# Dense up products: one matmul of 512 columns for both sides of the tokens, with a copy and a sum behind each group

## The chip, the cores and the metric

One core of one Trainium2 chip. The metric is device time in microseconds (us), from the start of the program on the core to its end. The kernel before ran three times: 1690.91 us in the median, 1690.83 to 1691.85. One further execution was profiled. It took 1693.8 us, of which 1691.8 us are the span from the first instruction to the last; all rows below come from it.

## The reference, cut to what matters

A decoder trunk of two layers over 256 tokens with 1024 features. Each layer has a mixer (attention and a recurrent branch), a feed-forward part and a small gated embedding. In layer 0 the feed-forward part is dense, in layer 1 it is a choice of experts. Only the dense one is touched:

```python
def swiglu(x, w1, w3, w2):
    return (jax.nn.silu(x @ w1) * (x @ w3)) @ w2

xn2 = rmsnorm(h, ffn_norm[0])
h = h + swiglu(xn2, dense_w1, dense_w3, dense_w2)   # w1, w3: 1024 x 3584, w2: 3584 x 1024
```

All data are 32-bit floats. The kernel keeps that precision on TensorE (PE) by splitting each operand into a rounded part ("hi") and its remainder ("lo") and adding three products: hi x hi, hi x lo and lo x hi.

## The kernel before, in words

**Weights.** SyncE (SP) loads weights from HBM in chunks of 2 MB into a ring of three slots `raw` (`load`, line 568); a chunk can be loaded when the chunk three before it has been split. A chunk is four quarters. The list `quarters` (line 148) names them in the order of their use. ScalarE (ACT) rounds quarter g into `w_hi` (`split_hi`, line 471), VectorE (DVE) subtracts to give `w_lo` (`split_lo`, line 482). There are six buffers of each, so the rounding of quarter g waits until the quarter g-6 has been read by PE (`wait_read`, line 457). Both engines call their splits through `Line.to(end)` (class `Line`, line 692), which emits the splits that are not yet emitted, up to but without the index `end`. So the place of a call of `hi.to` or `lo.to` in an engine's program is where its splits stand in that engine's order, and what is written ahead of them comes ahead of them.

**The dense part.** The 3584 hidden features are 7 chunks (c) of 4 tiles (ft), 28 groups. For each group i = 4c + ft PE multiplies one quarter of w1 and one of w3, eight k-tiles each, with the normed tokens, into the two halves of one PSUM bank: 2 x 8 x 3 matmuls of 256 columns (`split_product`, line 1175: `w_hi` with `xn_hi`, `w_hi` with `xn_lo`, `w_lo` with `xn_hi`). Groups take two banks `work` in turn. After the four groups of chunk c, PE multiplies with the four quarters of w2 of chunk c-1 (`down`, line 1337, 96 matmuls of 256 columns into `acc`), after the seventh chunk also with its own (`last_down`, line 1345). So the quarters stand in the order: eight of w1 and w3, (from the second chunk on) four of w2 of the chunk before, eight of w1 and w3, and so on.

**What follows a group** (`dense`, lines 950 and 1968; `last` is the index of the group's w3 quarter):

- ACT: `hi.to(last + 5)`; at the first group the root of the norm; wait for the scaled group; silu; `hi.to(last + 7)`.
- DVE: `lo.to(last + 5)`; at the first group the reciprocal of the root; wait for the group; multiply the bank of 512 columns by `rinv` into `up_buf` (line 1977; the profile names that space `gate_b`), which frees the bank; `lo.to(last + 7)`; wait for the silu; multiply, round to `hid_hi`, subtract to `hid_lo` (lines 1984, 1986, 1988).

Between groups of one chunk `last` grows by 2, so that `to(last + 5)` finds nothing left and `to(last + 7)` emits two quarters. Over w2's four quarters `last` jumps by 6: at the first group of the third to seventh chunk (c = 2 to 6) `to(last + 5)` emits four quarters, those of the groups ft = 1 and ft = 2 of that chunk. The group ft = 0 itself has its two quarters from before.

**The norm.** The root that the scaling needs is made from a sum that PE writes to the bank `misc` right after group 0 (`norm_root`, lines 1181, 767, 1732). The eight tiles `xn_hi` and `xn_lo` are made while the mixer's last products (`out`, eight groups of 24 matmuls) end; DVE adds each `out` bank to `hT`, which frees the bank.

Of the kernel before, what the change touches and what calls it, by code (L numbers as in the profile page):

```python
# [8 lines left out]
F32 = mybir.dt.float32  # L9
# [6 lines left out]
P = 128  # L16
D = 1024
T = 256
# [91 lines left out]
def trunk(nc, xT, pT, cols, rows, relT, wrg_d, wig_d, router_d, mix_w, dense_w, moe_w, ple_w, ple_p, bias_line, outT):  # L110
    groups = []
    for l in range(DEPTH):
        groups += [(l, *g) for g in mixer_groups()]
        if l % 2 == 0:
            groups += [(l, "ffn", c, ft) for c in range(FC) for ft in range(FT)]
        groups += [(l, "ple", j) for j in range(KT)]

    own = {g: (2 + TT * (g[2] - 1) + g[3], g[0]) for g in groups if g[1] == "qkv" and g[2]}
# [54 lines left out]
    with ExitStack() as ctx:  # L173
# [6 lines left out]
        def shared(name, n):  # L180

            with nc.sbuf_tensor(name, [P, n], F32) as plain:
                pass
            return plain, sb(name + "_r", [P, n], F32R)
# [3 lines left out]
        w_hi = [sb(f"w_hi{i}", [P, QUARTER], F32R) for i in range(UNITS_HELD)]  # L188
        w_lo = [sb(f"w_lo{i}", [P, QUARTER], F32R) for i in range(UNITS_HELD)]
        hT = sb("hT", [P, KT, T])  # L190
        x1, x1_r = shared("x1", KT * T)
        x2, x2_r = shared("x2", KT * T)
        areaA, areaA_r = shared("areaA", KT * T)
        areaB, areaB_r = shared("areaB", KT * T)
        areaK = sb("areaK", [P, KT * T])
# [60 lines left out]
        def squares_of(n):  # L256
            return areaA[:, 0:KT * T] if n % 3 == 0 else spare[:, KT * T:2 * KT * T]

        work_ps = [ctx.enter_context(nc.psum_tensor(f"work{i}", [P, 512], F32)) for i in range(2)]
        acc = [ctx.enter_context(nc.psum_tensor(f"acc{i}", [P, 1024], F32)) for i in range(2)]  # L260
        pv_ps = ctx.enter_context(nc.psum_tensor("pv_ps", [P, 512], F32))
        misc = ctx.enter_context(nc.psum_tensor("misc", [P, 512], F32))
        quad = [acc[0][:, 0:512], acc[0][:, 512:1024], acc[1][:, 0:512], acc[1][:, 512:1024]]
        work = [work_ps[0][:, :], work_ps[1][:, :]] + quad

        score_ps = acc[0][:, :].rearrange("p (h s) -> p h s", h=2)

# [31 lines left out]
        renormed = sem("renormed")  # L299
        ffn_bank = sem("ffn_bank")  # L300
        scaled = sem("scaled")
        ple_scaled = sem("ple_scaled")
        logits_taken = sem("logits_taken")
        logits_turned = sem("logits_turned")
# [152 lines left out]
        def wait_read(eng, g):  # L457

            l, _, _, _, by = quarters[g]
            if by[0] == "qkv":  # L460
                _, c, q = by
                if q < 3:
                    eng.wait_ge(rows_used, 9 * l + 3 * c + q + 1)
                else:
                    wait_full(eng, l, "qkv", c, TT - 1)
            elif by[0] == "w2":
                eng.wait_ge(ffn_acc, FC * FT * (l // 2) + FT * by[1] + by[2] + 1)
            else:
                wait_full(eng, l, *by)
# [24 lines left out]
        def wait_full(eng, l, *g):  # L494
            b, n = place[(l, *g)]
            eng.wait_ge(work_full[b], n + 1)

        def wait_taken(eng, l, *g):
            b, n = place[(l, *g)]
# [248 lines left out]
        def _(act):  # L748
# [201 lines left out]
            def dense(l):  # L950
                for i in range(FC * FT):
                    c, ft = divmod(i, FT)
                    last = q_at[((l, "w3", c), ft)]
                    hi.to(last + 5)
                    if i == 0:
                        norm_root(3 * l + 1)
                    act.wait_ge(scaled, FC * FT * (l // 2) + i + 1)
                    a = up_buf[:, i % 2, 0, :]
                    act.activation(a, a, ACT.Silu).then_inc(silu_ok, 1)
                    hi.to(last + 7)  # L960
                hi.to(phase_q[(l, "ple")] + 2)
                for k in range(KT):
                    if k == 6:
                        hi.to(phase_q[(l, "ple")] + 4)
                    norm_piece(3 * l + 2, k)
                hi.to(phase_q[(l, "ple")] + 5)
# [194 lines left out]
        def _(pe):  # L1161
# [167 lines left out]
            def dense(l):  # L1329
                def down_part(c, ft, j):  # L1330
                    g = q_at[((l, "w2", c), ft)]
                    hi, lo = unit(w_hi, g), unit(w_lo, g)
                    return split_product(quad[j // 2][:, T * (j % 2):T * (j % 2) + T], (hi[:, j, :], lo[:, j, :]),
                                         (hid_hi[:, c % 2, ft, :], hid_lo[:, c % 2, ft, :]),
                                         c == 0 and ft == 0 and j % 2 == 0, c == FC - 1 and ft == FT - 1)

                def down(c):
                    pe.wait_ge(hid_ok, FC * FT * (l // 2) + FT * (c + 1))
                    for ft in range(FT):
                        need(q_at[((l, "w2", c), ft)])  # L1340
                        for j in range(KT):
                            mm = down_part(c, ft, j)
                        mm.then_inc(ffn_acc, 1)

                def last_down():

                    c = FC - 1
                    for b in range(4):
                        for ft in range(FT):
                            if b == 0:  # L1350
                                pe.wait_ge(hid_ok, FC * FT * (l // 2) + FT * c + ft + 1)
                                need(q_at[((l, "w2", c), ft)])
                            for j in (2 * b, 2 * b + 1):
                                mm = down_part(c, ft, j)
                            if b == 3:
                                mm.then_inc(ffn_acc, 1)
                        if b < 3:
                            mm.then_inc(ffn_bank, 1)

                for c in range(FC):  # L1360
                    for ft in range(FT):
                        out = group_open(l, "ffn", c, ft)
                        for half, w in enumerate(("w1", "w3")):
                            g = q_at[((l, w, c), ft)]
                            need(g)
                            hi, lo = unit(w_hi, g), unit(w_lo, g)
                            for k in range(KT):
                                if c == 0 and ft == 0 and half == 0:
                                    pe.wait_ge(normed, KT * split_count(3 * l + 1) + k + 1)
                                mm = split_product(out[:, T * half:T * half + T], (hi[:, k, :], lo[:, k, :]),  # L1370
                                                   (xn_hi[:, k, :], xn_lo[:, k, :]), k == 0, k == KT - 1)
                        group_close(mm, l, "ffn", c, ft)
                        if c == 0 and ft == 0:
                            norm_root(3 * l + 1)
                    if c:
                        down(c - 1)
                last_down()
# [281 lines left out]
        def _(dve):  # L1659
# [308 lines left out]
            def dense(l):  # L1968
                for i in range(FC * FT):
                    c, ft = divmod(i, FT)  # L1970
                    last = q_at[((l, "w3", c), ft)]
                    lo.to(last + 5)
                    if i == 0:
                        norm_root(3 * l + 1)
                    wait_full(dve, l, "ffn", c, ft)
                    up = up_buf[:, i % 2, :, :]
                    taken(dve.tensor_tensor(up, bank_of(l, "ffn", c, ft).rearrange("p (h t) -> p h t", h=2),  # L1977
                                            rinv[:, :].unsqueeze(1).to_broadcast([P, 2, T]), ALU.mult), l, "ffn", c, ft)
                    wait_taken(dve, l, "ffn", c, ft)
                    dve.sem_inc(scaled, 1)  # L1980
                    lo.to(last + 7)
                    dve.wait_ge(silu_ok, FC * FT * (l // 2) + i + 1)
                    s = up[:, 0, :]
                    step(dve.tensor_tensor(s, s, up[:, 1, :], ALU.mult))
                    step.settle()
                    step(dve.tensor_copy(hid_hi[:, c % 2, ft, :], s))
                    step.settle()
                    dve.tensor_tensor(hid_lo[:, c % 2, ft, :], s, hid_hi[:, c % 2, ft, :].bitcast(F32),
                                      ALU.subtract).then_inc(hid_ok, 1)
                lo.to(phase_q[(l, "ple")] + 2)  # L1990
                for b in range(4):
                    if b < 3:
                        dve.wait_ge(ffn_bank, 3 * (l // 2) + b + 1)
                    else:
                        dve.wait_ge(ffn_acc, FC * FT * (l // 2 + 1))
                    dve.tensor_tensor(hT[:, 2 * b:2 * b + 2, :], hT[:, 2 * b:2 * b + 2, :],
                                      quad[b].rearrange("p (k t) -> p k t", k=2), ALU.add).then_inc(h_ffn, 1)
                    if b:
                        norm_piece(3 * l + 2, b - 1)
                norm_piece(3 * l + 2, 3)  # L2000
                lo.to(phase_q[(l, "ple")] + 5)
# [398 lines left out]
```

## Time and profile before

| | |
|---|---|
| median of 3 runs | 1690.91 us (1690.83 to 1691.85) |
| profiled execution | 1693.8 us, its span 1691.8 us |
| PE busy | 1671.0 us, 99% of the span |
| DVE, ACT busy | 1076.2 us (64%), 883.0 us (52%) |
| granted PE clock, mean over the span | 0.996 |
| dense part | about 250.4 to 494.4 us in the span |

PE is busy nearly everywhere. Matmuls overlap in their records, so that a busy PE does not say how fast they follow each other; for that one takes the distance of two starts. "x24" in a row means that 24 like instructions in a row were merged into one. "[3.38 <-PE work L1179]" means that the engine sat idle for 3.38 us before the instruction and what ended it. The clock is in shares of full speed (2.4 GHz).

### The profile page before, as it was taken

What the parts mean: (1) busy time and instruction counts of PE and PEld (TensorE: products, weight loads), DVE (VectorE), ACT (ScalarE), POOL (GpSimd) and SP (SyncE); (2) the same over time, 40 slices, a digit from 0 to 9 for tenths busy, and PEclk for the clock granted to TensorE, in tenths of its full rate; (3) what the DMA queues carried; (4) which work ended last, traced back from release to release, by engine and by line L of the source; (5) the groups of instructions that cost most, each with busy time, mean ns of one, the idle gap of its engine ahead of it and who ended that gap; (6) DMA issues with size and microseconds to landing.
All of it is one profiled execution on the core that took longest, in us unless ns stands there. A gap on an engine that the chain in (4) does not pass through costs nothing.

```text
span 1691.8 us, 26030 instructions
## 1 busy us (share of the span) xinstructions
PE 1671.0 (99%) x10246; PEld 1299.1 (77%) x10246; DVE 1076.2 (64%) x1662; ACT 883.0 (52%) x1349; POOL 18.6 (1%) x51
## 2 busy tenths in 40 slices
PE   9999999999999999998999999999999999999998
PEld 8888999999998988996666666666656666566557
DVE  7697876665668897866554555545555455555456
ACT  6778643433356678534534444445444455454444
POOL 3000000000000000000000000000000000000000
PEclk9999999999999999998999999999999999999999
DMA  9342453633544442435999999999999999999990
GB/s 336 144 163 100 166 215 153 243 153 150 210 188 150 156 157 106 170 156 190 417 417 388 417 412 409 418 392 414 410 410 417 412 394 410 411 417 413 394 383 27
DMA packets 62320, 485.98 MB, mean 287 GB/s; under 512 B 6880, under 2 KB 9200, under 8 KB 11504
## 3 DMA queue, kind: packets, MB, share of 16 engines
q1 hardware_dynamic: 62016, 484.09, 71.5%
q8 instruction: 84, 1.38, 0.3%
q14 instruction: 44, 0.36, 0.1%
q10 hardware_dynamic: 176, 0.15, 0.0%
HBM read 483.15 MB, written 1.07 MB: 286 GB/s over the span
## 4 chain that ended last, share of the span: by engine, by line
PE 95%; DVE 2%; DMA 1%; ACT 1%; issue 1%; POOL 0%; DVEq 0%; ACTq 0%; POOLq 0%
PE work L1177 17%; PE work L1178 16%; PE work L1179 16%; PE acc L1526 12%; PE acc L1177 6%; PE acc L1552 6%; PE acc L1179 6%; PE acc L1178 6%; PE acc L1258 1%; PE pv_ps L1488 1%; PE misc L1444 1%; PE misc L1442 1%; PE acc L1271 1%; PE misc L1426 1%; PE acc L1296 1%; PE misc L1435 1%
## 5 line engine op out<-in xcount | busy, mean ns | idle before, releaser
L2215 DVE TENSOR_TENSOR w_lo<-raw,w_hi 128x1024 fp32r<-128x1024 f32 x288 | 339.7, 1221 | 191.9 <-ACT w_hi L1005 186.6
L485 DVE TENSOR_TENSOR w_lo<-raw,w_hi 128x1024 fp32r<-128x1024 f32 x236 | 283.9, 1219 | 89.4 <-ACT w_hi L480 87.5
L1005 ACT ACTIVATE w_hi<-raw 128x1024 fp32r<-128x1024 f32 x288 | 288.2, 1050 | 55.0 <-DMA raw<-in_moe_w 51.6
L1177 PE MATMUL work<-x_r,w_hi 128*128 128x256 f32 x1024 | 297.0, 290 | 1.2 <-DVE gate_b L1977 0.7
L1178 PE MATMUL work<-x_r,w_hi 128*128 128x256 f32 x1024 | 289.5, 283 | 0.0
L1179 PE MATMUL work<-x_r,w_lo 128*128 128x256 f32 x1024 | 289.4, 283 | 0.0
L480 ACT ACTIVATE w_hi<-raw 128x1024 fp32r<-128x1024 f32 x236 | 241.8, 1048 | 67.8 <-PE acc L1179 29.1
L1526 PE MATMUL acc<-raw,bias 128*64 128x512 f32 x768 | 204.5, 598 | 0.0
L1177 PEld LDWEIGHTS work<-x_r,w_hi 128*128 128x128 f32 x1024 | 196.0, 191 | 8.9 <-issue 6.2
L1178 PEld LDWEIGHTS work<-x_r,w_hi 128*128 128x128 f32 x1024 | 196.1, 192 | 1.0 <-issue 0.7
L1179 PEld LDWEIGHTS work<-x_r,w_lo 128*128 128x128 f32 x1024 | 196.1, 192 | 0.0
L1177 PE MATMUL work<-w_hi,bias_r 128*128 128x512 f32 x448 | 182.7, 408 | 2.7 <-DVE w_lo L2215 2.7
L1178 PE MATMUL work<-w_lo,bias_r 128*128 128x512 f32 x448 | 175.7, 392 | 0.0
L1179 PE MATMUL work<-w_hi,bias_r 128*128 128x512 f32 x448 | 175.2, 391 | 0.0
L1526 PEld LDWEIGHTS acc<-raw,bias 128*64 128x64 f32 x768 | 58.6, 136 | 93.9 <-issue 93.9
L1177 PEld LDWEIGHTS work<-w_hi,bias_r 128*128 128x128 f32 x448 | 84.7, 189 | 41.2 <-issue 24.7
L1016 ACT ACTIVATE bias_r<-pv_ps 128x512 fp32r<-128x512 f32 x28 | 16.7, 597 | 171.2 <-PE pv_ps L1488 171.2
L1179 PEld LDWEIGHTS work<-w_hi,bias_r 128*128 128x128 f32 x448 | 84.7, 189 | 18.1
L1178 PEld LDWEIGHTS work<-w_lo,bias_r 128*128 128x128 f32 x448 | 84.8, 189 | 16.1
L1177 PE MATMUL acc<-w_hi,bias_r 128*128 128x512 f32 x224 | 93.3, 417 | 2.2 <-DVE w_lo L2215 2.2
L1552 PE MATMUL acc<-raw,lru 128*64 128x512 f32 x384 | 88.4, 598 | 0.0
L1179 PE MATMUL acc<-w_hi,bias_r 128*128 128x512 f32 x224 | 88.0, 393 | 0.0
(350 smaller groups left out, 2782.5 us busy)
## 6 DMA issues: line engine op xcount, KB each, us to landing
raw<-in_moe_w SPq DMA_DIRECT2D x288, 1024.0 KB, 10.5
raw<-in_mix_w SPq DMA_DIRECT2D x33, 2048.0 KB, 8.0
x<-in_moe_w SPq DMA_DIRECT2D x48, 1024.0 KB, 10.7
raw<-in_dense_w SPq DMA_DIRECT2D x21, 2048.0 KB, 8.2
raw<-in_ple_w SPq DMA_DIRECT2D x4, 2048.0 KB, 10.9
raw<-in_mix_w SPq DMA_DIRECT2D x4, 512.0 KB, 7.3
areaK<-in_ple_p SPq DMA_DIRECT2D x2, 1024.0 KB, 10.2
hT<-in_xT SPq DMA_DIRECT2D x4, 256.0 KB, 6.5
```

The source lines that it names most:

```text
L480: act.activation(unit(w_hi, g), raw_part(g), ACT.Copy).then_inc(hi_ok, 1)
L485: eng.tensor_tensor(unit(w_lo, g), raw_part(g), unit(w_hi, g).bitcast(F32), ALU.subtract).then_inc(split_ok, 1)
L1005: act.activation(w_hi[n % UNITS_HELD][:, :], heavy_quarter(where, c, j), ACT.Copy).then_inc(m_hi_ok, 1)
L1177: pe.matmul(out, stat[0], move[0], start=start, stop=False, skip_group_check=True)
L1178: pe.matmul(out, stat[0], move[1], start=False, stop=False, skip_group_check=True)
L1179: return pe.matmul(out, stat[1], move[0], start=False, stop=stop, skip_group_check=True)
L1258: mm = pe.matmul(score_ps[:, hh, 0:w], qT[HD * hh:HD * hh + HD, t, b * P:(b + 1) * P], kTT[HD * hh:HD * hh + HD, t // 2, 0:w], start=True, ...
L1271: mm = pe.transpose(acc[1][:, o:o + P], ebuf[:, u % 2, hh, P * kt:P * kt + P], ident[:, :])
L1296: mm = pe.matmul(quad[c % 4][HD * b:HD * b + HD, T * n:T * n + T], w[HD * b:HD * b + HD, c, :], xcT[HD * b:HD * b + HD, c, :], start=True, ...
L1526: mm = pe.matmul(quad[2][LIGHT * b:LIGHT * b + LIGHT, :], xg_light[:, k, :], w, start=(k == 0), stop=(k == KT - 1), skip_group_check=True)
L1552: mm = pe.matmul(quad[3][LIGHT * b:LIGHT * b + LIGHT, :], l_hid[:, ft, :], w, start=(c == 0 and ft == 0), stop=(c == FC - 1 and ft == FT - ...
L2215: dve.tensor_tensor(w_lo[u][:, :], heavy_quarter(where, n // HEAVY_C, n % HEAVY_C), w_hi[u][:, :].bitcast(F32), ALU.subtract).then_inc(m_s ...
```

## The change

Three things change, all for the dense part of layer 0:

1. `x1` and `x2`, which hold `xn_hi` and `xn_lo`, become halves of one buffer, so that one matmul can read both as 2 x 256 moving columns. For each quarter and k-tile PE now runs `w_hi` on [`xn_hi`, `xn_lo`] (512 columns) and `w_lo` on `xn_hi` (256 columns).
2. A group's result is now two sides of 256 columns for each of w1 and w3: 1024 columns, two banks. Even groups use both `work` banks, odd ones the banks of `pv_ps` and `misc`. ACT copies the second side to `up_buf`, DVE adds the first side to it (which frees the banks), then multiplies by `rinv`.
3. ACT and DVE put this copy, sum and scaling ahead of `to(last + 5)`, except at group 0. PE waits for both last `out` banks ahead of group 0, for the root (`rooted`) ahead of group 1, as that group writes to `misc`, and from group 2 on for the sum of the group two before.

```diff
-        x1, x1_r = shared("x1", KT * T)
-        x2, x2_r = shared("x2", KT * T)
+        x12, x12_r = shared("x12", 2 * KT * T)
+        x1, x1_r = x12[:, 0:KT * T], x12_r[:, 0:KT * T]
+        x2, x2_r = x12[:, KT * T:], x12_r[:, KT * T:]
+        xn_both = x12_r[:, :].rearrange("p (s k t) -> p k s t", s=2, k=KT)
...
+        def ffn_sides(i):
+            return (work_two, side_two)[i % 2][:, :].rearrange("p (h s t) -> p h s t", h=2, s=2)
...
 # ScalarE
                 for i in range(FC * FT):
                     c, ft = divmod(i, FT)
                     last = q_at[((l, "w3", c), ft)]
+                    if i == 0:
+                        hi.to(last + 5)
+                        norm_root(3 * l + 1)
+                    act.wait_ge(ffn_full, FC * FT * (l // 2) + i + 1)
+                    if i >= 2:
+                        act.wait_ge(hid_ok, FC * FT * (l // 2) + i - 1)
+                    act.activation(up_buf[:, i % 2, :, :], ffn_sides(i)[:, :, 1, :], ACT.Copy).then_inc(ffn_sided, 1)
                     hi.to(last + 5)
-                    if i == 0:
-                        norm_root(3 * l + 1)
                     act.wait_ge(scaled, FC * FT * (l // 2) + i + 1)
                     a = up_buf[:, i % 2, 0, :]
                     act.activation(a, a, ACT.Silu).then_inc(silu_ok, 1)
                     hi.to(last + 7)
...
 # TensorE
+                def up_product(out, hi, lo, k):
+                    pe.matmul(out[:, :, :], hi, xn_both[:, k, :, :], start=(k == 0), stop=False, skip_group_check=True)
+                    return pe.matmul(out[:, 0, :], lo, xn_hi[:, k, :], start=False, stop=(k == KT - 1), skip_group_check=True)
+
+                wait_taken(pe, l, "out", KT - 2)
+                wait_taken(pe, l, "out", KT - 1)
                 for c in range(FC):
                     for ft in range(FT):
-                        out = group_open(l, "ffn", c, ft)
+                        i = FT * c + ft
+                        if i == 1:
+                            pe.wait_ge(rooted, 3 * l + 2)
+                        elif i:
+                            pe.wait_ge(ffn_summed, FC * FT * (l // 2) + i - 1)
+                        out = ffn_sides(i)
...
-                                mm = split_product(out[:, T * half:T * half + T], (hi[:, k, :], lo[:, k, :]),
-                                                   (xn_hi[:, k, :], xn_lo[:, k, :]), k == 0, k == KT - 1)
-                        group_close(mm, l, "ffn", c, ft)
+                                mm = up_product(out[:, half, :, :], hi[:, k, :], lo[:, k, :], k)
+                        mm.then_inc(ffn_full, 1)
...
 # VectorE
+                    if i == 0:
+                        lo.to(last + 5)
+                        norm_root(3 * l + 1)
+                    up = up_buf[:, i % 2, :, :]
+                    both = ffn_sides(i)
+                    dve.wait_ge(ffn_sided, FC * FT * (l // 2) + i + 1)
+                    dve.tensor_tensor(up, up, both[:, :, 0, :], ALU.add).then_inc(ffn_summed, 1)
+                    dve.wait_ge(ffn_summed, FC * FT * (l // 2) + i + 1)
+                    dve.tensor_tensor(up, up, rinv[:, :].unsqueeze(1).to_broadcast([P, 2, T]), ALU.mult).then_inc(scaled, 1)
                     lo.to(last + 5)
-                    if i == 0:
-                        norm_root(3 * l + 1)
-                    wait_full(dve, l, "ffn", c, ft)
-                    up = up_buf[:, i % 2, :, :]
-                    taken(dve.tensor_tensor(up, bank_of(l, "ffn", c, ft).rearrange("p (h t) -> p h t", h=2),
-                                            rinv[:, :].unsqueeze(1).to_broadcast([P, 2, T]), ALU.mult), l, "ffn", c, ft)
-                    wait_taken(dve, l, "ffn", c, ft)
-                    dve.sem_inc(scaled, 1)
                     lo.to(last + 7)
```

## Rows read from the trace of the kernel before

**Rows 1.** The page's chain that ended last, shares by engine.

```profile
PE 95%; DVE 2%; DMA 1%; ACT 1%; issue 1%; POOL 0%; DVEq 0%; ACTq 0%; POOLq 0%
```

**Rows 2.** Windows, mid dense part: us, PE, PEld, DVE, ACT, POOL, PEclk, DMA, GB/s.

```profile
340.00:370.00 30.00, 30.00 (x252) 30.00 (x252) 16.76 (x23) 10.61 (x15) 0.00 (x0) 1.00 0.44 166
```

**Rows 3.** Timeline of PE: a matmul of group 24, and the first of group 25.

```profile
452.75 0.28 PE L1179 MATMUL work<-x_r,w_lo 128*128 128x256 f32 x1
...
453.95 0.28 PE L1177 MATMUL work<-x_r,w_hi 128*128 128x256 f32 x1
```

**Rows 4.** Timeline of PE in layer 1's first products, matmuls of 512 columns.

```profile
542.80 0.39 PE L1178 MATMUL acc<-w_lo,gate_a_r 128*128 128x512 f32 x1
...
544.61 0.39 PE L1177 MATMUL acc<-w_hi,gate_a_r 128*128 128x512 f32 x1
```

**Rows 5.** Timeline of DVE over a down product and the first group behind it.

```profile
442.46 2.56 DVE L485 TENSOR_TENSOR w_lo<-raw,w_hi 128x1024 fp32r<-128x1024 f32 x2
446.67 1.23 DVE L485 TENSOR_TENSOR w_lo<-raw,w_hi 128x1024 fp32r<-128x1024 f32 x1 [1.65 <-ACT w_hi L480]
449.55 1.23 DVE L485 TENSOR_TENSOR w_lo<-raw,w_hi 128x1024 fp32r<-128x1024 f32 x1 [1.65 <-ACT w_hi L480]
454.15 0.69 DVE L1977 TENSOR_TENSOR gate_b<-work,rinv 128x512 f32<-128x512 f32 x1 [3.38 <-PE work L1179]
```

**Rows 6.** Timeline of ACT over the same stretch.

```profile
437.98 2.94 ACT L480 ACTIVATE w_hi<-raw 128x1024 fp32r<-128x1024 f32 x3
...
448.45 1.06 ACT L480 ACTIVATE w_hi<-raw 128x1024 fp32r<-128x1024 f32 x1 [1.82 <-PE acc L1179]
454.94 0.42 ACT L959 ACTIVATE gate_b<-gate_b 128x256 f32<-128x256 f32 x1 [5.42 <-DVEq L1980]
```

**Rows 7.** ACT's copies of 512 columns from PSUM, by source line: min/median/max ns.

```profile
L1016 ACT ACTIVATE bias_r<-pv_ps x28: 597/597/597, 798.3 to 1629.9; 128x512 fp32r<-128x512 f32 x28
```

**Rows 8.** Timeline, all engines, opening of the dense part.

```profile
250.75 0.42 DVE L1963 TENSOR_TENSOR hT<-hT,work 128x256 f32<-128x256 f32 x1 [1.32 <-PE work L1179]
...
253.02 0.39 PE L1177 MATMUL work<-x_r,w_hi 128*128 128x256 f32 x1
...
256.98 0.47 PE L1177 MATMUL work<-x_r,w_hi 128*128 128x256 f32 x1
...
257.37 0.47 ACT L778 ACTIVATE spare<-misc,small 128x256 f32<-128x256 f32 x1 [2.67 <-PE misc L1188]
```

**Rows 9.** The chain in order of time, 256 to 276 us: start, us, what.

```profile
263.10 8.09 DMA raw<-in_dense_w
```

**Rows 10.** Timeline of DVE, one turn of its loop in chunk 0.

```profile
280.14 0.68 DVE L1977 TENSOR_TENSOR gate_b<-work,rinv 128x512 f32<-128x512 f32 x1
282.31 2.36 DVE L485 TENSOR_TENSOR w_lo<-raw,w_hi 128x1024 fp32r<-128x1024 f32 x2 [1.49 <-ACT w_hi L480]
284.59 0.42 DVE L1984 TENSOR_TENSOR gate_b<-gate_b 128x256 f32<-128x256 f32 x1
...
285.71 0.68 DVE L1977 TENSOR_TENSOR gate_b<-work,rinv 128x512 f32<-128x512 f32 x1
```

**Rows 11.** Timeline of ACT in the same turn.

```profile
280.91 0.42 ACT L959 ACTIVATE gate_b<-gate_b 128x256 f32<-128x256 f32 x1 [3.25 <-DVEq L1980]
281.23 1.99 ACT L480 ACTIVATE w_hi<-raw 128x1024 fp32r<-128x1024 f32 x2
```

**Rows 12.** Timeline of PE, two idle stretches at the start of layer 1's experts.

```profile
765.99 0.39 PE L1624 MATMUL misc<-gate_a 128*128 128x8 f32 x2 [2.65 <-DVE gate_a L2054]
...
780.59 0.77 PE L1177 MATMUL work<-w_hi,bias_r 128*128 128x512 f32 x1 [2.73 <-DVE w_lo L2215]
```

**Rows 13.** Windows of PE there: us, PE busy (x), PEclk, DMA, GB/s.

```profile
764.00:766.00 2.00, 0.01 (x1) 1.00 0.01 4
...
768.00:769.00 1.00, 0.94 (x6) 0.70 0.00 0
...
771.00:772.00 1.00, 1.00 (x7) 0.60 0.00 0
...
778.00:779.00 1.00, 0.00 (x0) 0.82 1.04 434
...
785.00:786.00 1.00, 1.00 (x5) 0.77 0.98 393
```

More of the change, by code:

```diff
@@ L113, in trunk @@
         groups += [(l, *g) for g in mixer_groups()]
-        if l % 2 == 0:
-            groups += [(l, "ffn", c, ft) for c in range(FC) for ft in range(FT)]
         groups += [(l, "ple", j) for j in range(KT)]
@@ L257, in squares_of @@
             return areaA[:, 0:KT * T] if n % 3 == 0 else spare[:, KT * T:2 * KT * T]
-        work_ps = [ctx.enter_context(nc.psum_tensor(f"work{i}", [P, 512], F32)) for i in range(2)]
+        work_two = ctx.enter_context(nc.psum_tensor("work", [P, 1024], F32))
         acc = [ctx.enter_context(nc.psum_tensor(f"acc{i}", [P, 1024], F32)) for i in range(2)]
-        pv_ps = ctx.enter_context(nc.psum_tensor("pv_ps", [P, 512], F32))
-        misc = ctx.enter_context(nc.psum_tensor("misc", [P, 512], F32))
+        side_two = ctx.enter_context(nc.psum_tensor("side", [P, 1024], F32))
+        pv_ps, misc = side_two[:, 0:512], side_two[:, 512:1024]
         quad = [acc[0][:, 0:512], acc[0][:, 512:1024], acc[1][:, 0:512], acc[1][:, 512:1024]]
-        work = [work_ps[0][:, :], work_ps[1][:, :]] + quad
+        work = [work_two[:, 0:512], work_two[:, 512:1024]] + quad
         score_ps = acc[0][:, :].rearrange("p (h s) -> p h s", h=2)
@@ L301, in trunk @@
         scaled = sem("scaled")
+        ffn_full = sem("ffn_full")
+        ffn_sided = sem("ffn_sided")
+        ffn_summed = sem("ffn_summed")
         ple_scaled = sem("ple_scaled")
@@ L465, in wait_read @@
                     wait_full(eng, l, "qkv", c, TT - 1)
+            elif by[0] == "ffn":
+                eng.wait_ge(ffn_full, FC * FT * (l // 2) + FT * by[1] + by[2] + 1)
             elif by[0] == "w2":
```

## The prediction

> **What bounds the kernel now.** I read first the chain that ended last, then the windows of the dense part, then the timelines of the three engines at three places: a steady chunk, the opening, the first two chunks. 95% of the chain is PE [rows 1], and in the middle of the dense part PE is busy 30.00 of 30.00 us, at full clock, while DVE has 13 us and ACT 19 us to spare [rows 2]. So two things count: how fast PE's matmuls follow each other, and whether PE will have to wait where it does not wait now.
>
> Pace: between 452.75 and 453.95 lie ten matmuls of 256 columns, 0.120 us each [rows 3]. The matmuls of 512 columns in layer 1's first products follow at (544.61 - 542.80) / 8 = 0.226 us [rows 4]. A group is 48 x 0.120 = 5.76 us, a down product 96 x 0.120 = 11.52 us, a chunk of four groups and one down product 34.56 us. From the end of group 24, 453.95, this leads back to 315.71 for the end of group 8 and 298.43 for that of group 7.
>
> Slack: at 437.98 ACT begins three splits, of which two belong to `to(last + 7)` of the group before; the third, and three more up to 448.45, are the four of `to(last + 5)` for the next chunk [rows 6]. DVE does their halves from 443.6 to 450.8 [rows 5]. All this lies beside PE's down product (about 436.7 to 448.2) and group 24 (to 453.95); afterwards DVE sits idle 3.38 us for group 24's end [rows 5]. Here is the spare time that now keeps PE fed.
>
> **The change part by part.**
>
> *The matmuls.* Of 48 per group 16 pairs of 256 columns become 16 of 512. A pair saves 0.240 - 0.226 = 0.014 us, a group 0.22 us, so a group takes 5.54 us. The columns stay the same; 256 more of them cost 0.226 - 0.120 = 0.106 us, so that 0.014 us of each matmul do not grow with its columns [rows 3, 4], and that is what is saved. The Trainium skill (TensorE: Matmul & The Clock Gate, section "Back-to-back issue gap") gives only about 2.5 ns for this at full clock; by it all 28 groups would save 1.1 us, where the rows give 6.2. The rows disagree with it, and the sum goes by them.
>
> *The order, c = 2 to 6.* At the first group of these chunks the four splits now stand behind the copy and the scaling, and so behind the end of that very group. Group ft = 1 needs the first of them. Let E be when PE could start it (453.95 in rows 3). An engine sees the group's end at E + 0.20 (454.15) [rows 3, 5]. ACT's copy from PSUM of 512 columns takes 0.60 us [rows 7], to E + 0.80. DVE's sum reads PSUM and SBUF as the scaling did, 0.69 us [rows 5], from E + 0.85 to 1.54. The multiplication behind it has as many elements, 0.69 us, to E + 2.23; ACT's rounding of the first quarter, 1.06 us [rows 6], has ended by then (E + 1.85). Then DVE's remainder, 1.23 us [rows 5], to E + 3.46, and 0.05 us to PE. A first matmul after a wait delays the next by some 0.1 us more. So PE stands 3.6 us, five times: +18.0 us. The next quarters come 1.15 us apart and are wanted 2.8 us apart, so no second wait follows. Bounds of one stall: 2.5 us (0.2 + 1.06 + 1.23, if the three added operations cost nothing in the chain) and 4.2 us (the two DVE passes and the copy with 0.2 us more each). I take 3.6, the sum of the nearest rows.
>
> *The added passes.* ACT gets 28 x 0.60, DVE 28 x 0.69 us. In the chunks c = 2 to 6 they are covered by the slack of rows 2 and, once a chunk, by the down product of 11.5 us. In chunks 0 and 1 they are not: DVE's loop already runs without a pause, 5.57 us from one scaling to the next: 280.14, the silu at 280.91, roundings from 281.23, remainders 282.31, products 284.59, next 285.71 [rows 10, 11]. With another 0.71 us (pass and semaphore) its turn is 6.28 us, over the 5.54 of a group, and with two pairs of banks PE is held to it.
>
> *Opening.* PE must wait for the last `out` bank, 250.75 + 0.42 [rows 8], so it starts at 251.2 and not 250.4. But it stood until 253.02 for the last normed tiles anyway; that takes up the delay, and group 0 ends at 256.8 as before. Group 1, which ran from 256.98, now waits for the root, 257.37 + 0.47: 257.9 [rows 8], +0.9 us. That is taken up too, because the fourth chunk's load starts only when quarter 6 is split: 263.10 + 8.09 = 271.19 [rows 9]. This split lies behind the reciprocal and now one more pass, 0.7 us; its successor pays another pass before group 3. So group 3's sum begins at 280.14 + 0.7 + 0.7 = 281.54. Group 5 opens on it at 282.3, then 288.6, 294.9 at DVE's pace, and group 7 ends at 300.4 against 298.43: +2.0 us. The down product then gives DVE time to catch up.
>
> *Moved but free.* The loads wait for split quarters. In c = 2 to 6 the latest one is issued some 9 us after the first group's end and has to be there two groups later; with 8.1 us for a load [rows 9] it is in time. The smaller buffers' merging costs nothing: same bytes, same reads. `side` holds `misc` and `pv_ps`, which no one else uses until the next norm.
>
> *Sum.* +2.0 (to group 7) - 20 x 0.22 = -4.4 (groups 8 to 27) + 18.0 = **+15.6 us** without the clock.
>
> *The clock.* Now PE idles 3.5 us five times, where rows of before have no such stop in this part. Nearest rows: PE idled 2.65 us up to 765.99 with the clock at 1.00; it fell after it, at about 768.4, amid short matmuls, and was back about 771.8. In the stop of 2.73 us that ends at 780.59 it fell at about 778.6 and came back at about 785.5 [rows 12, 13]. The first fall cost half of 3.4 us, 1.7 us; the second half of the work from 780.59 to 785.5, 2.4 us. So between 0 and 5 falls, 0 to +12 us. One of two shorter stops held the fall within it; I take two falls of five at 1.7 us, as dense matmuls follow at once here: +3.4 us. Total **+19.0 us**: 1693.8 + 19.0 = 1712.8 against the profiled execution, 1709.9, say **1710**, against the median, which lies 2.9 us under the profiled one.
>
> **The rivals.**
>
> *A, the clock holds in all stops:* +15.6 us, 1706.5. For it: the stop of 2.65 us, through which the clock stayed at 1.00. Against it: the fall at 778.6 within a shorter one. 0.26.
>
> *B, it falls in all five:* +15.6 + 5 x (1.7 to 2.4), 1715 to 1718.5. These stops are longer than both in rows 12. The Trainium skill (same page, section "Why this matters for your kernels") says that idle gaps between bursts of matmuls of about this length put the clock back to its lower level; by that rule B is the outcome. The trace agrees in one stop and not in the other. 0.13.
>
> *C, no gain from wider matmuls:* the 0.226 of rows 4 is from a run of 512 only; mixed with 256 the saving of 4.4 may be nothing, then 1714. By the skill's 2.5 ns it would be nearly so. 0.05.
>
> *D, the other side:* PE is not starved at ft = 1. Its place is the end of the first group of each chunk from c = 2 on; it decides if the stop there is under (4.4 - 2.0) / 5 = 0.5 us. Then +2.0 - 4.4 = -2.4 us, 1688.5; and if DVE's longer turn in chunks 0 and 1 were hidden as well, 28 x 0.22 = 6.2 us are gained, 1684.7. It would need the four splits to be issued ahead of the wait. `Line.to` emits in program order, and the one rounding and one remainder alone are 2.3 us [rows 5, 6]. 0.03 for 1688.5, 0.02 for 1684.7.
>
> **How the numbers follow.** The forecast, one to three falls, has 0.51. About 0.2%, 3.4 us, is what a measurement of this kernel can tell from no change. Slower by more than that are the forecast, A, B and C: 0.95; within it the first form of D: 0.03; faster: 0.02. The range: without falls and with a stall 0.7 us shorter 15.6 - 3.5 = +12, 1703; up to four falls of 2.4 us and a little on the chain, +26, 1717.
>
> **What would show each step.** In the profile of the changed kernel PE should sit idle about 3.5 us, five times, some 37 us apart, released by DVE's `w_lo`, each right behind a chunk's first group. DVE's idle time ahead of its first PSUM operation there stays, and its four splits stand behind that group and not beside the down product. Matmuls of 512 and 256 columns start 0.226 and 0.120 us apart. In chunks 0 and 1 PE waits for DVE's sum (`gate_b`), with turns of 6.3 us. PEclk shows whether it fell, and how often. The dense part should last about 263 us instead of 244. I am wrong if those five stops are missing or last under 0.5 us, if the turn in chunk 1 is not over 6 us, or if the gain per group is far from 0.22 us.

## Result and profile after

The changed kernel takes 1717.2 us in the median of four runs (1714.35 to 1720.89), the kernel before 1691.4 us beside it: the ratio is 1.0149, with a 95% interval of 1.0137 to 1.0161, so 25 us more. It is slower, as forecast, but at the very top of the range of 1703 to 1717 us: by the ratio, 1690.91 x 1.0149 = 1716.1 us, and the median itself is 1717.2. The profiled execution took 1720.9 us, 27.1 more than that of before; its span is 1719.0 us, 27.2 more.

Two lines of the page: the chain that ended last (against rows 1), and the wide matmuls of the odd groups (line, engine, operation, busy us, mean ns, idle before, released by):

```profile
PE 93%; DVE 4%; ACT 1%; issue 1%; DMA 1%; POOL 0%; ACTq 0%; DVEq 0%; POOLq 0%
...
L1377 PE MATMUL side<-x_r,w_hi 128*128 128x512 f32 x224 | 89.0, 434 | 18.1 <-DVE w_lo L490 16.8
```

DVE has gained two points on the chain, and the odd groups (`side`) stood idle for `w_lo`. The waits of PE in the dense part of the changed kernel (who for whom, us in total, times, longest):

```profile
PE side L1377 <- DVE w_lo L490: 16.8, 5, 3.4
PE work L1377 <- DVE gate_b L2005: 2.2, 2, 1.9
PE side L1377 <- DVE gate_b L2005: 0.7, 2, 0.4
PE side L1377 <- ACT spare L787: 0.6, 1, 0.6
PE work L1377 <- issue: 0.6, 1, 0.6
```

Five stops for the quarter of group ft = 1, four waits for DVE's sum (line 2005) in chunks 0 and 1, one for the root, and one of 0.6 us ahead of group 0, where PE now waits for the `out` banks: all in parts where waits were forecast. The first of the five, in the timeline of PE (start, duration, instruction, idle before):

```profile
317.94 0.28 PE L1378 MATMUL work<-x_r,w_lo 128*128 128x256 f32 x1
321.58 0.47 PE L1377 MATMUL side<-x_r,w_hi 128*128 128x512 f32 x1 [3.36 <-DVE w_lo L490]
321.89 0.28 PE L1378 MATMUL side<-x_r,w_lo 128*128 128x256 f32 x1
...
326.00 0.39 PE L1377 MATMUL side<-x_r,w_hi 128*128 128x512 f32 x1
```

Without the stop the next matmul would have started 0.12 us after 317.94. It starts 3.52 us later than that, and its successor comes 0.31 us behind it and not 0.23: 3.60 us for the stop. The chain in it, from the timelines of ACT and DVE:

```profile
318.26 0.60 ACT L970 ACTIVATE gate_b<-work 128x512 f32<-128x512 f32 x1 [7.61 <-PE work L1378]
318.75 3.89 ACT L485 ACTIVATE w_hi<-raw 128x1024 fp32r<-128x1024 f32 x4
```

```profile
318.89 0.69 DVE L2005 TENSOR_TENSOR gate_b<-gate_b,work 128x512 f32<-128x512 f32 x1 [5.67 <-ACT gate_b L970]
319.61 0.69 DVE L2007 TENSOR_TENSOR gate_b<-gate_b,rinv 128x512 f32<-128x512 f32 x1
320.22 6.90 DVE L490 TENSOR_TENSOR w_lo<-raw,w_hi 128x1024 fp32r<-128x1024 f32 x6
```

Where rows 5 and 6 show the four splits beside the down product, ACT now begins them at 318.75 and DVE at 320.22, behind the group. DVE idled 5.67 us before it. The first remainder is done at 321.5, and PE starts. The clock in two of the stops (windows of PE: us, busy (x), PEclk, DMA, GB/s):

```profile
321.00:322.00 1.00, 0.42 (x2) 1.00 0.00 0
322.00:323.00 1.00, 1.00 (x7) 0.72 0.00 0
...
325.00:326.00 1.00, 1.00 (x5) 0.58 0.00 0
...
360.00:361.00 1.00, 0.18 (x1) 0.50 0.00 0
...
366.00:367.00 1.00, 1.00 (x6) 0.60 1.08 229
```

After the first stop it fell at 322.4, with PE at work again, and was back at 325.8. In the second it fell at 360.0, still within the stop, and was back at 366.8. The other three stops, in wider windows:

```profile
398.00:410.00 12.00, 9.04 (x43) 0.86 0.32 109
438.00:450.00 12.00, 10.08 (x43) 0.72 0.40 145
478.00:490.00 12.00, 9.93 (x50) 0.86 0.38 138
```

At half clock a mean of 0.86 over 12 us is 3.4 us of it, one of 0.72 some 6.8. So in this execution it fell at all five, three times for 3.4 us and twice for 6.8.

**Where the 27.2 us went**, from these timelines. This execution reached the dense part 0.8 us earlier (-0.8). To the end of group 7 it lost 3.3 us. The stops took 5 x 3.60 = 18.0. Twenty groups gained 3.2 us: 9 at 0.21 (ft = 1 to 3 of the chunks c = 3, 4 and 6) and 11 at 0.11, see below. The starts of the chunks' first sums lie 39.23, 40.15, 38.96 and 40.14 us apart, where four groups, a down product and a stop make 37.7 (c = 2 and 5) or 37.4 (c = 3 and 4). The rest is the clock: 1.5, 2.7, 1.5 and 2.4 us, with 1.3 in the last chunk 9.5 us. That makes 26.8; the other 0.4 us came behind the dense part.

### The profile page after: what moved, and what is told of

The parts are those of the page before. It is cut to its first block, busy times and chain, and to the rows that moved or that the text cites. A ratio compares the mean times of both kernels' runs of the same rounds, so it can differ in the third digit from the quotient of the medians.

```text
span 1719.0 us, 25189 instructions
## 1 busy us (share of the span) xinstructions
PE 1679.3 (98%) x9798; PEld 1282.7 (75%) x9798; DVE 1093.1 (64%) x1690; ACT 897.2 (52%) x1377; POOL 19.5 (1%) x51
## 4 chain that ended last, share of the span: by engine, by line
PE 93%; DVE 4%; ACT 1%; issue 1%; DMA 1%; POOL 0%; ACTq 0%; DVEq 0%; POOLq 0%
PE work L1192 14%; PE work L1193 13%; PE work L1194 13%; PE acc L1553 12%; PE acc L1192 6%; PE acc L1579 6%; PE acc L1194 6%; PE acc L1193 6%; PE side L1377 3%; PE work L1377 2%; PE side L1378 1%; PE work L1378 1%; PE side L1469 1%; PE side L1471 1%; PE acc L1273 1%; PE side L1515 1%
## 5 line engine op out<-in xcount | busy, mean ns | idle before, releaser
L1192 PE MATMUL work<-x_r,w_hi 128*128 128x256 f32 x576 | 169.8, 295 | 0.4 <-DVE x_r L1740 0.4
L1193 PE MATMUL work<-x_r,w_hi 128*128 128x256 f32 x576 | 162.8, 283 | 0.0
L1194 PE MATMUL work<-x_r,w_lo 128*128 128x256 f32 x576 | 162.6, 282 | 0.0
L1192 PEld LDWEIGHTS work<-x_r,w_hi 128*128 128x128 f32 x576 | 110.0, 191 | 7.6 <-issue 6.2
L1193 PEld LDWEIGHTS work<-x_r,w_hi 128*128 128x128 f32 x576 | 110.2, 191 | 1.0 <-issue 0.7
L1194 PEld LDWEIGHTS work<-x_r,w_lo 128*128 128x128 f32 x576 | 110.1, 191 | 0.0
L1377 PE MATMUL side<-x_r,w_hi 128*128 128x512 f32 x224 | 89.0, 434 | 18.1 <-DVE w_lo L490 16.8
L1031 ACT ACTIVATE bias_r<-side 128x512 fp32r<-128x512 f32 x28 | 16.7, 597 | 171.2 <-PE side L1515 171.2
L1192 PE MATMUL acc<-w_hi,bias_r 128*128 128x512 f32 x224 | 93.4, 417 | 2.2 <-DVE w_lo L2243 2.2
```

The source lines that it names most:

```text
L1192: pe.matmul(out, stat[0], move[0], start=start, stop=False, skip_group_check=True)
L1193: pe.matmul(out, stat[0], move[1], start=False, stop=False, skip_group_check=True)
L1194: return pe.matmul(out, stat[1], move[0], start=False, stop=stop, skip_group_check=True)
L1377: pe.matmul(out[:, :, :], hi, xn_both[:, k, :, :], start=(k == 0), stop=False, skip_group_check=True)
```

## The experiments

All times are compared with the kernel before on the same chip.

**1. The splits ahead again.** Wide matmuls, copy and sum stay; the order goes back.

```diff
                         norm_root(3 * l + 1)
+                    hi.to(last + 5)
                     act.wait_ge(ffn_full, FC * FT * (l // 2) + i + 1)
...
-                    hi.to(last + 5)
                     act.wait_ge(scaled, FC * FT * (l // 2) + i + 1)
...
+                    lo.to(last + 5)
                     up = up_buf[:, i % 2, :, :]
...
-                    lo.to(last + 5)
                     lo.to(last + 7)
```

> The changed kernel with the four splits back ahead of the copy and the sum on both engines (to(last + 5) first), the wide matmuls kept. Theory 1 (the order makes the five stops of 3.4 to 3.5 us, and these the falls of the clock): no stop behind the first groups, no fall in the dense part, so 18 us and some 10 us go and what is left is the opening (+3.2 us to the end of group 7) less the wider matmuls (20 groups at 0.10 to 0.22 us): 1690 to 1692.5 us, same as before. Rival (the stops come from the copy and the sum themselves, or from the banks shared with other tiles): stops of over 1 us stay, over 1700 us.

1693.1 us (11 runs), ratio 1.0005 (0.9996 to 1.0014). PE's waits in the dense part:

```profile
PE work L1377 <- DVE gate_b L2006: 2.1, 2, 1.8
PE side L1377 <- DVE gate_b L2006: 0.6, 2, 0.3
PE side L1377 <- ACT spare L787: 0.6, 1, 0.6
```

The five stops are gone, and the clock stayed at 1.00 in the dense part. Two calls moved, one on each engine, are worth 24 us. The median lies 0.6 us over the expected 1690 to 1692.5. What is left is that the wide matmuls about pay for the opening.

**2. The order alone**, on the kernel before with its narrow matmuls: ACT waits for the group ahead of `hi.to(last + 5)`, DVE scales it ahead of `lo.to(last + 5)`, except at group 0.

```diff
...
+                    wait_full(act, l, "ffn", c, ft)
                     hi.to(last + 5)
                     act.wait_ge(scaled, FC * FT * (l // 2) + i + 1)
...
                     dve.sem_inc(scaled, 1)
+                    lo.to(last + 5)
                     lo.to(last + 7)
```

> The kernel before with its narrow matmuls and no copy or sum, only to(last + 5) moved behind the group's end (ACT waits for the group, DVE scales it first). Theory 1: five stops of 0.2 + 1.06 + 1.23 + 0.1, about 2.6 us, are 13 us, and the clock adds 0 to 10 us: 1704 to 1714. If falls of the clock need stops of over 3 us, 1704. Rival (order alone costs nothing): 1691.

1712.6 us (four runs, 1710.5 to 1713.1), ratio 1.0121 (1.0106 to 1.0137). The first of its five stops, PE's timeline:

```profile
318.67 0.36 PE L1179 MATMUL work<-x_r,w_hi 128*128 128x256 f32 x1 [2.50 <-DVE w_lo L485]
```

The clock around the five stops (windows of PE as above):

```profile
316.00:326.00 10.00, 7.50 (x51) 0.83 0.21 52
354.00:364.00 10.00, 7.50 (x63) 1.00 0.16 32
392.00:402.00 10.00, 7.50 (x63) 1.00 0.20 51
426.00:438.00 12.00, 9.51 (x69) 0.86 0.10 19
466.00:476.00 10.00, 7.50 (x63) 1.00 0.01 2
```

2.50 us idle, as the rounding and the remainder make it. With the slower first matmul that is 13 us; in the profiled execution the clock fell at two of the five for 3.4 us each. So the order needs neither the copy nor the wide matmuls to cost most of the loss, and the clock fell also at stops of 2.5 us, though not at each.

**3. Longer stops.** Two more DVE passes ahead of the sum, on the changed kernel, at these five groups only; their output is used by nothing.

```diff
...
+                    if c >= 2 and ft == 0:
+                        for _ in range(2):
+                            step(dve.tensor_tensor(silu_buf, up, rinv[:, :].unsqueeze(1).to_broadcast([P, 2, T]), ALU.mult))
+                            step.settle()
                     dve.tensor_tensor(up, up, both[:, :, 0, :], ALU.add).then_inc(ffn_summed, 1)
```

> The changed kernel with two more DVE passes of 512 elements ahead of the sum, at the five first groups only (their output is not used). Stops grow by 1.4 us to 4.9 us: +7 us by the stops alone. Theory 3 (whether the clock falls is decided by the length of the stop): it falls in all five in every run, and longer: 1724 to 1732 with less spread. Rival (it falls by chance, whatever the length between 3.4 and 4.9): 1722 to 1728 with runs as far apart as in the changed kernel (6.5 us).

1726.4 us (1726.19 to 1728.14), ratio 1.0201 (1.0185 to 1.0216). The waits of PE and the clock around four of the stops:

```profile
PE side L1377 <- DVE w_lo L490: 24.1, 5, 4.8
```

```profile
360.00:370.00 10.00, 6.07 (x26) 0.83 0.12 25
398.00:410.00 12.00, 7.18 (x31) 0.72 0.08 14
438.00:450.00 12.00, 7.19 (x31) 0.72 0.00 0
478.00:490.00 12.00, 7.19 (x31) 0.73 0.00 0
```

In this execution the clock fell at every stop, three times for 6.8 us. Each run's own mean clock tells how long it was low over the whole span, 2 x (1 - clock) x span: 38 to 45 us in these four runs, 21 to 38 us in the changed kernel's four, 21 to 24 us with stops of 2.5 us, 7 to 14 us in the kernel before. The low time was longer with the longer stops, and the runs lie closer (2 us apart and not 6.5). But it differs from run to run with the same stops, most of all in the changed kernel, whose slowest run was low for 37.8 us and its fastest for 20.5. The 7 to 14 us of the kernel before lie outside the dense part (in its profiled execution the clock first fell at 768.4). By that, an estimate, the changed kernel's fastest run was low for 7 to 14 us in the dense part, two to four times 3.4. With four runs each these are tendencies; what decides a single fall was not tested.

**4. Rounding before the silu.** As experiment 1, and ACT rounds the two later quarters right behind its copy.

```diff
...
                     act.activation(up_buf[:, i % 2, :, :], ffn_sides(i)[:, :, 1, :], ACT.Copy).then_inc(ffn_sided, 1)
+                    hi.to(last + 7)
                     act.wait_ge(scaled, FC * FT * (l // 2) + i + 1)
                     a = up_buf[:, i % 2, 0, :]
                     act.activation(a, a, ACT.Silu).then_inc(silu_ok, 1)
-                    hi.to(last + 7)
```

> As the kernel with the splits ahead, and ACT rounds the two later quarters between its copy and the silu, so that DVE need not wait 1.43 us for them after the scaling. Theory 2 (chunks 0 and 1 are held by DVE's turn of 6.24 us): the turn falls to about 4.9 us, under a group's 5.6, PE waits for no sum from group 5 on, and the load of the fourth chunk starts some 1.5 us sooner: 1685.5 to 1688. Rival (it is the load alone that holds them, or the silu now comes late): 1690 to 1692 like the kernel with the splits ahead.

1689.8 us (11 runs), ratio 0.9986 (0.9977 to 0.9995): 0.14% less than the kernel before. One turn of DVE in the changed kernel in chunk 0, and one here:

```profile
281.93 0.68 DVE L2005 TENSOR_TENSOR gate_b<-gate_b,side 128x512 f32<-128x512 f32 x1
282.64 0.69 DVE L2007 TENSOR_TENSOR gate_b<-gate_b,rinv 128x512 f32<-128x512 f32 x1
284.77 2.36 DVE L490 TENSOR_TENSOR w_lo<-raw,w_hi 128x1024 fp32r<-128x1024 f32 x2 [1.43 <-ACT w_hi L485]
...
288.17 0.68 DVE L2005 TENSOR_TENSOR gate_b<-gate_b,work 128x512 f32<-128x512 f32 x1
```

```profile
277.53 0.68 DVE L2006 TENSOR_TENSOR gate_b<-gate_b,side 128x512 f32<-128x512 f32 x1
278.24 0.69 DVE L2008 TENSOR_TENSOR gate_b<-gate_b,rinv 128x512 f32<-128x512 f32 x1
278.86 2.35 DVE L490 TENSOR_TENSOR w_lo<-raw,w_hi 128x1024 fp32r<-128x1024 f32 x2
...
282.24 0.68 DVE L2006 TENSOR_TENSOR gate_b<-gate_b,work 128x512 f32<-128x512 f32 x1
```

6.24 us against 4.71: the 1.43 us in which DVE waited for ACT are gone, and PE waits for no sum any more. The time itself missed the expected 1685.5 to 1688, by 1.8 us in the median and 0.8 in the profiled execution (1688.8): the turn shortened as expected, but it was worth less.

**5. The same order on the kernel before.** Narrow matmuls, roundings before the silu (`wait_full` and `hi.to(last + 7)` ahead of the wait for `scaled`).

> The kernel before with narrow matmuls, and ACT rounds the two later quarters before the silu instead of behind it. It tells whether the 2.2 us that the kernel with roundings before the silu gains over the kernel before come from the wide matmuls or from that order. If from the wide matmuls (28 groups at 0.11 us less the wait for the root): here only PE's wait of about 0.7 us before group 4 goes, 1690.5 to 1692. If from the order: 1689 to 1690.

1692.1 us (11 runs), ratio 0.9998 (0.9989 to 1.0007). The order alone gives nothing that can be measured. The two intervals overlap a little, but the profiles agree with the reading that the gain of experiment 4 is that of the wide matmuls, once what they brought with them is out of PE's way: from c = 2 on a chunk takes 34.12 us there and 34.56 us here, four groups of 0.11 us less.

**6. One stretch.** As experiment 4, with `xn_hi` and `xn_lo` side by side for each k-tile, so that the 512 moving columns lie in one stretch of memory. The views of the two halves follow suit.

```diff
-        xn_both = x12_r[:, :].rearrange("p (s k t) -> p k s t", s=2, k=KT)
+        xn_both = x12_r[:, :].rearrange("p (k s t) -> p k s t", s=2, k=KT)
...
```

> As the kernel with roundings before the silu, with xn_hi and xn_lo interleaved by k-tile, so that the 512 moving columns lie in one stretch of memory and not in two of 256 that are 2048 elements apart. A pair of matmuls took 0.353 us where 0.226 + 0.120 = 0.346 was forecast. Theory 4 (the two stretches cost 7 ns): 0.346 here and 28 x 16 x 0.007 = 3.1 us less, about 1686.6. Rival (the stretches cost nothing, it is how matmuls of 512 and 256 follow each other): 0.353, 1689.8.

1689.3 us (11 runs), ratio 0.9985 (0.9976 to 0.9994), where experiment 4 had 0.9986: no difference. Pairs of its matmuls:

```profile
320.03 0.40 PE L1378 MATMUL work<-x_r,w_hi 128*128 128x512 f32 x1
320.26 0.28 PE L1379 MATMUL work<-x_r,w_lo 128*128 128x256 f32 x1
320.38 0.40 PE L1378 MATMUL work<-x_r,w_hi 128*128 128x512 f32 x1
...
321.79 0.40 PE L1378 MATMUL work<-x_r,w_hi 128*128 128x512 f32 x1
```

(321.79 - 320.03) / 5 = 0.352 us. The two stretches were not the cause.

**7. Wide ones first, then narrow ones**, eight and eight for each quarter, as experiment 4 otherwise.

```diff
...
-                                mm = up_product(out[:, half, :, :], hi[:, k, :], lo[:, k, :], k)
+                                up_product(out[:, half, :, :], hi[:, k, :], None, k)
+                            for k in range(KT):
+                                mm = up_product(out[:, half, :, :], None, lo[:, k, :], k)
```

> As the kernel with roundings before the silu, with the eight wide matmuls of a quarter first and then its eight narrow ones, so that 512 and 256 columns no longer alternate. If alternation costs the 7 ns: wide ones follow at 0.226 and narrow ones at 0.120, 0.346 for a pair, about 1686.6. If not: 0.353 for a pair, 1689.8.

1688.9 us (11 runs), ratio 0.9984 (0.9975 to 0.9993). Rows of PE, eight merged into one:

```profile
319.96 1.12 PE L1379 MATMUL side<-x_r,w_lo 128*128 128x256 f32 x8
320.91 2.00 PE L1378 MATMUL work<-x_r,w_hi 128*128 128x512 f32 x8
322.75 1.12 PE L1379 MATMUL work<-x_r,w_lo 128*128 128x256 f32 x8
```

Eight of each take 322.75 - 319.96 = 2.79 us, 0.349 for a pair, about halfway between the two expected values. The wide ones follow at 1.84 / 8 = 0.230, the narrow ones at 0.119. The difference in time from experiment 4 is within the intervals.

**8. The root not awaited.** As experiment 4, but group 1 goes to the idle banks `acc`, and the wait for the root stands before group 3.

```diff
-            return (work_two, side_two)[i % 2][:, :].rearrange("p (h s t) -> p h s t", h=2, s=2)
+            return (acc[0] if i == 1 else (work_two, side_two)[i % 2])[:, :].rearrange("p (h s t) -> p h s t", h=2, s=2)
...
-                        if i == 1:
+                        if i == 3:
                             pe.wait_ge(rooted, 3 * l + 2)
-                        elif i:
+                        if i > 1:
                             pe.wait_ge(ffn_summed, FC * FT * (l // 2) + i - 1)
```

> As the kernel with roundings before the silu, with group 1 in the idle banks acc, so that PE need not wait for the root before it. If that wait of 0.6 us plus a slow first matmul (0.1) is on PE's path to the end: 1689.0, 0.7 to 0.9 us less. If PE then waits elsewhere (the load of the fourth chunk comes at a time of its own, group 4 needs it): 1689.8, no difference.

1690.0 us (11 runs), ratio 0.9989 (0.998 to 0.9998): no difference from experiment 4. The wait of 0.6 us is gone, and in the profiled execution (1693.3 us, the slowest of the eleven) PE waited at group 4 in its place, for a sum behind the load of the fourth chunk:

```profile
276.22 0.50 PE L1377 MATMUL work<-x_r,w_hi 128*128 128x512 f32 x1 [1.55 <-DVE gate_b L2005]
```

## Why the prediction was right, point by point

**The five stops** were right in place, length and cause: forecast 3.6 us each, 18.0 in all, measured 3.60. Experiment 1 takes them away by the order alone, experiment 2 makes them by the order alone. Rival D has fallen.

**The clock** is the term that was mis-sized. The forecast took two falls of five at 1.7 us, +3.4. The profiled execution had all five, three of 1.3 to 1.5 us and two of 2.4 and 2.7: 9.5 us, which is rival B with its price of 8.5 to 12 us. The other three runs were low for 20.5 to 34.3 us and not 37.8, so that they had fewer or shorter falls, the fastest perhaps as few as the forecast had. The median lies inside B's 1715 to 1718.5 all the same, because the rest of the sum was too small too. The step that failed is "One of two shorter stops held the fall within it; I take two falls of five at 1.7 us". What counts is also a fall that comes after the stop, as the one at 322.4 did, and the stop of 2.65 us in rows 12 was itself followed by one at 768.4; read so, both shorter stops spoke for B. But that fall stands 2.4 us behind the stop, amid short matmuls, and no run shows that the stop is its cause. The Trainium skill (TensorE: Matmul & The Clock Gate, section "Why this matters for your kernels") warns of idle gaps of about this length between bursts of matmuls; the trace of the changed kernel agrees, with a fall at each of five stops of 3.36 us. The shorter stops of 2.50 us in experiment 2 had falls too, at two of five.

**The wide matmuls** gained less than forecast: a pair took 0.353 us in most stretches and not 0.346, so a group gained 0.11 us and not 0.22, and the twenty groups 3.2 us and not 4.4. The saving that does not grow with columns was taken from a run of 512-column matmuls only. The 2.5 ns of the Trainium skill (the same page, section "Back-to-back issue gap") would have given 0.04 us for a group; the trace, with 0.11 in most groups and 0.21 in the others, lies between it and the rows. Rival C was half right for the groups at 0.353.

**The opening** cost 3.3 us to group 7 and not 2.0. Its places were right: the root (0.56 us idle), DVE's turn (forecast 6.28, measured 6.24), the load. The load itself took longer:

```profile
263.22 9.08 DMA raw<-in_dense_w
```

9.08 us against 8.09 [rows 9], and it moved all that hangs on it by 1.0 us. It took 9.01 and 9.15 us in experiments 1 and 3 too, and 8.00 in experiment 2 with its narrow matmuls. What makes the load longer was not tried.

**The sum without the clock** was +15.6 forecast and 3.3 + 18.0 - 3.2 = 18.1 measured. The two wrong sizes, -4.4 for -3.2 and +2.0 for +3.3, both went the same way. That the range held all the same was in part luck: its top stood for four falls of 2.4 us, 9.6 us, while the median run had some 7 to 8 us of the clock (an estimate: its 25.2 to 25.8 us more, less 18.1), and this covered most of the 2.5 us that the other two terms were short.

## What to carry to other kernels

Where a shared engine does both the evacuation of a group and the preparation of later work, look at where each wait stands ahead of preparation that could have gone on without it. Here a copy and a sum ahead of the splits turned the whole time of a down product into idle time of DVE and ACT, and moved their work to where PE needed it. And a stop of PE can cost more than its length: here five stops took 18.0 us themselves and 9.5 us more by the clock. Price the clock's fall with the stop, and count falls that come just after it.

## What was not expected of the hardware

The same pairs of 512 and 256 columns followed each other at two rates, 0.353 and 0.346 us, for a whole stretch of groups at a time, and changed between them only where something had broken the row of pairs: a stop, a fall of the clock, a down product, or the two matmuls of the norm's sum. In the changed kernel chunks c = 3, 4 and 6 ran their groups ft = 1 to 3 at 0.346, after a fall each, and those of c = 2 and 5 at 0.353, also after one; the first groups of all five ran at 0.353. The kernels of experiments 1, 4 and 6 stayed at 0.353 throughout; that of experiment 8 ran its groups 1 to 3 at 0.346, up to its stop, and the others at 0.353. Two stretches of memory are not the cause (experiment 6); alternation accounts for about half (experiment 7). What chooses the rate stays open.
